# Modulation groups in an attention stage: 64 matmuls moved to GpSimd arithmetic and two partition sums

## The reference

```
def modulation(cond, w_mod, b_mod):            # w_mod: 1024 x 6144
    m = jnp.einsum('bd,df->bf', jax.nn.silu(cond), w_mod) + b_mod
    return jnp.split(m[:, None, :], 6, axis=-1)
```

## Time and profile before

| | |
|---|---|
| median of 3 runs | 2192.92 us (2191.78 to 2200.79) |
| span of the profiled execution | 2192.0 us (the median of the runs is 0.9 us more) |
| TensorE busy | 2040.4 us, 93% |
| VectorE, ScalarE busy | 862.2 us (39%), 470.0 us (21%) |
| GpSimd busy | 154.5 us (7%), 147 instructions |
| mean granted clock of TensorE | 0.963 of full speed |
| the attention | 478 us to 849 us of the span |

### The profile page before, as it was taken

How to read it: one execution, slowest core, us unless ns; L and a number is a source line. 1 busy time by engine, 2 the same in 40 slices (tenths; PEclk the granted TensorE clock), 3 DMA queues, 4 the chain that set the end, 5 groups by cost and what they waited for, 6 DMA issues and landing times. The chain is left out here.

```text
span 2192.0 us, 27484 instructions
## 1 busy us (share of the span) xinstructions
PE 2040.4 (93%) x11455; PEld 1433.7 (65%) x11455; DVE 862.2 (39%) x1806; ACT 470.0 (21%) x927; POOL 154.5 (7%) x147
## 2 busy tenths in 40 slices
PE   5999999979999999999799999995998399999998
PEld 2776777755666665443587878782444387878785
DVE  2245345455666664337222222222546622222222
ACT  1222222126666563113000000001222100000000
POOL 0000000000000000001111111111000101111110
PEclk8999999989999999999899999997899699999999
DMA  9201111048544323753767878766221796878782
GB/s 355 91 25 48 41 44 41 25 108 272 182 178 167 135 97 107 274 170 140 269 235 259 304 259 301 253 214 227 84 82 72 261 343 239 302 260 303 260 287 61
DMA packets 159085, 404.29 MB, mean 184 GB/s; under 512 B 12561, under 2 KB 30664, under 8 KB 152818
## 3 DMA queue, kind: packets, MB, share of 16 engines
q1 hardware_dynamic: 142370, 344.30, 43.6%
q0 software_dynamic: 16592, 58.24, 9.2%
HBM read 339.46 MB, written 63.05 MB: 184 GB/s over the span
## 5 line engine op out<-in xcount | busy, mean ns | idle before, releaser
L1970 PE MATMUL experts_gu<-experts_h_t,shared_w_gate 128*128 128x160 f32 x2048 | 302.7, 301 | 4.1 <-issue 4.1
L1970 PEld LDWEIGHTS experts_gu<-experts_h_t,shared_w_gate 128*128 128x128 f32 x2048 | 288.7, 192 | 19.2 <-issue 19.2
L1970 PE MATMUL experts_gu<-experts_h_t,shared_w_up 128*128 128x160 f32 x2048 | 300.3, 300 | 0.0
L1970 PEld LDWEIGHTS experts_gu<-experts_h_t,shared_w_up 128*128 128x128 f32 x2048 | 286.6, 191 | 0.0
L2046 DVE TENSOR_TENSOR experts_hid<-experts_act,experts_gu 128x160 f32<-128x160 f32 x128 | 41.1, 321 | 479.4 <-ACT experts_act L2035 479.4
L1994 PE MATMUL experts_dn<-shared_w_down,experts_hid 128*128 128x512 f32 x512 | 225.8, 594 | 0.0
L523 PE MATMUL proj_cv<-proj_h_t,proj_w_in 128*128 128x256 f32 x960 | 214.0, 381 | 2.6 <-DVE proj_h_t L720 2.6
L2035 ACT ACTIVATE experts_act<-experts_gu 128x160 f32<-128x160 f32 x128 | 38.8, 303 | 813.4 <-PE experts_gu L1970 813.4
L523 PEld LDWEIGHTS proj_cv<-proj_h_t,proj_w_in 128*128 128x128 f32 x960 | 182.8, 192 | 29.3 <-issue 4.7
L1994 PEld LDWEIGHTS experts_dn<-shared_w_down,experts_hid 128*128 128x128 f32 x512 | 94.7, 190 | 113.8 <-issue 113.8
L1008 PE MATMUL attn_sc<-attn_keys_s,attn_q_s 96*128 96x512 f32 (+1 forms) x384 | 154.6, 539 | 3.8 <-DVE attn_pr_t L1141 2.8
(11 more groups left out here) (407 smaller groups left out, 2122.1 us busy)
## 6 DMA issues: line engine op xcount, KB each, us to landing
shared_w_gate<-w_gate_l SPq DMA_DIRECT2D x32, 2048.0 KB, 9.6
shared_w_up<-w_up_l SPq DMA_DIRECT2D x32, 2048.0 KB, 17.3
shared_w_down<-w_down_l SPq DMA_DIRECT2D x32, 2048.0 KB, 22.7
attn_w_mod<-w_mod_l SPq DMA_DIRECT2D x40, 1024.0 KB, 6.4
proj_w_in<-w_in_l SPq DMA_DIRECT2D x3, 2048.0 KB, 19.7
proj_x<-x POOLq DMA_DIRECT2D x10, 512.0 KB, 3.9
shared_w_down<-x SPq DMA_DIRECT2D x10, 512.0 KB, 4.4
layer_room_a<-w_mod_l SPq DMA_DIRECT2D x4, 1024.0 KB, 10.2
```

What stands on the lines that cost most here:

```text
L1970: last = pe.matmul(gu[j % 2][:, m * SLOTS:(m + 1) * SLOTS], w[u][:, k, j * P:(j + 1) * P], h_t[u][:, k, :], start=(k == 0), stop=(k == KD ...
```

## The change

Groups 3 and 4, (1, 1) and (1, 2), are no longer computed by steps of TensorE. GpSimd loads their blocks from its own DMA queue to two new buffers `w_sum`, multiplies each block by the column of conditioning values (a scalar for each partition) once for each of the two conditioning vectors, and adds the products up over the eight blocks to two sums of 128 x 2048: for a group 16 multiplications and 14 additions. TensorE then only sums the partitions of the two sums: `reduce`, eight matmuls of 512 columns with a stationary tile of 128 x 2 that holds ones in one column and zeros in the other, so that both sums land in the same rows as the steps' results did.

The reductions stand in slots 42 and 66, the turns of these groups in slots 44 and 68. Steps and turns of groups 0 to 2 stay where they were, and slots 39 to 57 lose their steps and turns. The sum of group 4 waits at its first block until the reduction of group 3 has read the sums (`sums_used`). The weights of the steps have two buffers in place of four, and VectorE writes four small columns of the selecting tile at the start.

```
--- before.py
+++ after.py
@@ -166,8 +166,10 @@
 
     WIDE, Q, R = 2048, 4, 32
 
-    def __init__(self, s, t, per, groups, bank, buffers, w=None, rows=2):
+    def __init__(self, s, t, per, groups, bank, buffers, w=None, rows=2, summed=()):
         self.t, self.per, self.groups, self.bank, self.NB = t, per, groups, bank, buffers
+        self.summed = list(summed)
+        self.stepped = [i for i in range(len(groups)) if i not in self.summed]
         self.w = w or [s.sb(f"w_mod{b}", [P, self.WIDE])[:] for b in range(buffers)]
         self.bias = [s.sb(f"mod_bias{u}", [P, BANK]) for u in range(rows)]
         self.rows = [s.sb(f"mod_rows{u}", [P, BANK]) for u in range(rows)]
@@ -175,7 +177,56 @@
         self.w_used, self.rows_ready, self.rows_out = s.sem("w_mod_used"), s.sem("mod_rows_ready"), s.sems("mod_rows_out", 2)
         self.zeroed, self.full = s.sem("mod_zeroed"), s.sem("mod_full")
         self.turned, self.columns = s.sem("mod_turned"), s.sem("mod_columns")
-        self.steps = KD * len(groups)
+        self.steps = KD * len(self.stepped)
+        if self.summed:
+            self.ws = [s.sb(f"w_sum{b}", [P, self.WIDE]) for b in range(2)]
+            self.sums = [s.sb(f"mod_sum{c}", [P, self.WIDE]) for c in range(2)]
+            self.scaled = s.sb("mod_scaled", [P, self.WIDE])
+            self.pick = s.sb("mod_pick", [P, 2, 2])
+            self.ws_in, self.sum_chain, self.sums_used = s.sems("w_sum_in", 2), s.sem("mod_sum_chain"), s.sem("mod_sums_used")
+            self.picked = s.sem("mod_picked")
+
+    def load_sum(self, pool, n):
+
+        if n < KD * len(self.summed):
+            (layer, g), k, b = self.groups[self.summed[n // KD]], n % KD, n % 2
+            pool.dma_start(self.ws[b][:], self.t[f"w_mod_l{layer}"][k * P:(k + 1) * P, g * self.WIDE:(g + 1) * self.WIDE]).then_inc(self.ws_in[b], 16)
+
+    def add_up(self, pool):
+
+        ch = Chain(pool, self.sum_chain)
+        for n in range(2):
+            self.load_sum(pool, n)
+        for n in range(KD * len(self.summed)):
+            j, k, b = n // KD, n % KD, n % 2
+            pool.wait_ge(self.ws_in[b], 16 * (n // 2 + 1))
+            if k == 0:
+                wait(pool, self.sums_used, j)
+            if k == 0:
+                for c in range(2):
+                    ch.add(pool.tensor_scalar(self.sums[c][:], self.ws[b][:], self.per.cond[:, k, c:c + 1], None, ALU.mult))
+                ch.settle()
+            else:
+                for c, scaled in ((0, self.scaled), (1, self.ws[b])):
+                    ch.link(pool.tensor_scalar(scaled[:], self.ws[b][:], self.per.cond[:, k, c:c + 1], None, ALU.mult))
+                    ch.add(pool.tensor_tensor(self.sums[c][:], self.sums[c][:], scaled[:], ALU.add))
+                ch.settle()
+            self.load_sum(pool, n + 2)
+
+    def reduce(self, pe, i):
+
+        j = self.summed.index(i)
+        pe.wait_ge(self.sum_chain, (4 * KD - 2) * (j + 1))
+        if j == 0:
+            pe.wait_ge(self.zeroed, 1 + len(self.bias))
+            pe.wait_ge(self.picked, 2)
+        wait(pe, self.rows_ready, i)
+        wait(pe, self.columns, self.turns_before(i))
+        for c in range(2):
+            for q in range(self.Q):
+                last = pe.matmul(self.bank[self.R * q:self.R * q + 2, :], self.pick[:, c, :], self.sums[c][:, q * BANK:(q + 1) * BANK],
+                                 start=(c == 0), stop=(c == 1), skip_group_check=True)
+        last.then_inc(self.sums_used, 1)
 
     def turns_before(self, i):
         return sum(1 for group in self.groups[:i] if self.wants_columns(group))
@@ -186,7 +237,7 @@
 
     def load(self, sp, n):
         if n < self.steps:
-            (layer, g), k, b = self.groups[n // KD], n % KD, n % self.NB
+            (layer, g), k, b = self.groups[self.stepped[n // KD]], n % KD, n % self.NB
             wait(sp, self.w_used, n - self.NB + 1)
             sp.dma_start(self.w[b], self.t[f"w_mod_l{layer}"][k * P:(k + 1) * P, g * self.WIDE:(g + 1) * self.WIDE]).then_inc(self.w_in[b], 16)
 
@@ -213,9 +264,14 @@
         dve.memset(self.bank, 0.0).then_inc(self.zeroed, 1)
         for u in range(len(self.bias)):
             dve.memset(self.bias[u][:], 0.0).then_inc(self.zeroed, 1)
+        if self.summed:
+            for c in range(2):
+                for m in range(2):
+                    last = dve.memset(self.pick[:, c, m:m + 1], 1.0 if c == m else 0.0)
+                last.then_inc(self.picked, 1)
 
     def step(self, pe, n):
-        i, k, b = n // KD, n % KD, n % self.NB
+        i, k, b = self.stepped[n // KD], n % KD, n % self.NB
         pe.wait_ge(self.w_in[b], 16 * (n // self.NB + 1))
         if k == 0:
             if i == 0:
@@ -235,7 +291,10 @@
             last.then_inc(self.turned, 1)
 
     def add_bias(self, dve, i):
-        dve.wait_ge(self.w_used, KD * (i + 1))
+        if i in self.summed:
+            dve.wait_ge(self.sums_used, self.summed.index(i) + 1)
+        else:
+            dve.wait_ge(self.w_used, KD * (self.stepped.index(i) + 1))
         dve.wait_ge(self.bias_in[i % 2], 16 * self.Q * (i // 2 + 1))
         if i >= 2:
             dve.wait_ge(self.rows_out[i % 2], 16 * self.Q * (i // 2))
@@ -897,7 +956,7 @@
         o_sb = [s.sb(f"o_sb{u}", [P, BANK]) for u in range(2)]
         sc = [s.ps(f"sc{b}", len(SPANS)) for b in range(2)]
         o_ps = s.ps("o")
-        mod = Modulation(s, t, per, [(0, 1), (0, 2), (1, 0), (1, 1), (1, 2)], s.ps("mod")[:], 4)
+        mod = Modulation(s, t, per, [(0, 1), (0, 2), (1, 0), (1, 1), (1, 2)], s.ps("mod")[:], 2, summed=(3, 4))
 
         vp_in, ks_in, vs_in = s.sem("vp_in"), s.sem("ks_in"), s.sem("vs_in")
         qs_in, o_out = s.sems("qs_in", 2), s.sems("o_out", 2)
@@ -921,10 +980,17 @@
         def last_pair(g):
             return 2 * g + 1 if g < 2 else (g - 1) * (HEADS // 2) + HEADS // 2 - 1
 
+        REDUCED_AT = {42: 3, 66: 4}
+
         def mod_tasks(n):
 
-            i, k = divmod((n - HEADS) // 2, KD // 2 + 1)
-            if n < HEADS or n % 2 == 0 or i >= len(mod.groups):
+            k = (n - HEADS) // 2
+            if n in REDUCED_AT:
+                return [("reduce", REDUCED_AT[n])]
+            if n - 2 in REDUCED_AT:
+                return [("turn", REDUCED_AT[n - 2])]
+            i, k = divmod(k, KD // 2 + 1)
+            if n < HEADS or n % 2 == 0 or i >= len(mod.stepped):
                 return []
             return [("step", KD * i + 2 * k), ("step", KD * i + 2 * k + 1)] if k < KD // 2 else [("turn", i)]
 
@@ -969,7 +1035,7 @@
                     for task, m in mod_tasks(n):
                         if task == "step":
                             mod.load(sp, m + mod.NB)
-                        else:
+                        elif task == "turn":
                             mod.store(sp, m)
                             mod.load_bias(sp, m + 2)
                     if n >= 2 and n % 2 == 0 and n // 2 - 1 == last_pair(group(n // 2 - 1)):
@@ -1054,10 +1120,16 @@
                     for task, m in mod_tasks(n):
                         if task == "step":
                             mod.step(pe, m)
+                        elif task == "reduce":
+                            mod.reduce(pe, m)
                         else:
                             mod.turn(pe, m)
                     if n + 2 < SLOTS_N:
                         scores(n + 2)
+
+            @block.gpsimd
+            def _(pool):
+                mod.add_up(pool)
 
             @block.scalar
             def _(act):
@@ -1154,6 +1226,8 @@
                     for task, m in mod_tasks(n):
                         if task == "step" and m % KD == KD - 1:
                             mod.add_bias(dve, m // KD)
+                        elif task == "reduce":
+                            mod.add_bias(dve, m)
                     if n + 2 < SLOTS_N:
                         guard(n + 2)
```

## The result

| | before | changed |
|---|---|---|
| median of 5 runs | 2192.92 us (2188.87 to 2200.79) | 2236.98 us (2233.63 to 2246.74) |
| ratio | | 1.0196, 95% interval 1.0172 to 1.0220 |
| span of the profiled execution | 2192.0 us | 2237.4 us |
| the attention, from its first matmul to the next stage's | 851.81 - 478.46 = 373.35 us | 895.81 - 478.31 = 417.50 us |

The kernel got slower by 44 us, and the attention alone by 44.15 us. The forecast was 2188.3 us with a range from 2185.5 to 2206.

The account below looks back on a forecast made before the run. TensorE, busy 93% of the span, was taken to bound the kernel. Span 2192.0 - 6.1 (TensorE's work) + 1.5 (transfers at the start) = 2187.4, plus 0.9 for the median: 2188.3 us, range 2185.5 to 2206.

Parts of the forecast that it names:

- TensorE's balance: TensorE in the attention: 10.9 us of steps removed, 3.7 us of reductions and 1.1 us of turns added, sum -6.1 us.
- The deadline: GpSimd's sum of group 4 has 116.7 us between the two reductions; anything beyond stops TensorE in slot 66.
- the start: First transfers of the attention: GpSimd's blocks beside the keys and the steps' blocks, taken to cost TensorE 1.5 us.
- The addition: One GpSimd addition of 128x2048 f32, priced at twice VectorE's 2.3 us: 4.6 us, 14 per group.
- The multiplication: One GpSimd multiplication by a column of scalars, 128x2048 f32, priced at VectorE's 2.3 us, 16 per group.
- high end: GpSimd's group with all 30 operations at twice VectorE's price, 4.6 us each, plus 7.5 us: 146 us; value taken 109.
- rival 4: Transfers at the attention's start cost 4 to 7 us in place of 1.5: kernel 2191 to 2194 us; chance 0.09.
- The two buffers: Step weights in two buffers, not four: loads hidden, cover 1.5 us at the worst, a miss costing that much each time.
- Rival 2: GpSimd multiplications cost 4.6 us like additions, group 146 us, TensorE stops 29 us in slot 66: 2218 us; chance 0.11.
- Rival 3: GpSimd and VectorE hinder each other in SBUF: one group up to 272 us, kernel 2405 us; chance 0.03.

## Why the prediction was wrong, point by point

- **TensorE's balance** was right: odd slots without steps take 3.90 us, a reduction 1.83, a turn 0.50 (0.56 forecast); 6.3 us gained where 6.1 were forecast, and 6.4 when measured alone.
- **The deadline** was right: 116.7 us forecast between the reductions, 116.3 measured. So was the place where it would show, slot 66. The 123 us a group at which the gain would be used up left out the 1.5 us of the start; with them it is 121.
- **The addition** was right: 4.6 us forecast, 4.53 measured.
- **The multiplication** is the step that failed. "Value taken: twice for the additions [...] and once for the multiplications, which fetch one": 2.3 us, with 4.6 as the high end. It takes 5.44 us. 16 x (5.44 - 2.3) = 50 us is all of the 48 by which the group's 157 exceed the 109 (additions, issues and handovers came out 2 us below their forecast). The high end of 146 us was itself too low, and the range of the time ended at 2206, that is at 134 us a group, with a chance of 0.14 left above it. My reasoning, that the price goes with the number of tensors fetched, is contradicted by the instruction itself: with one tensor and one operation it is dearer than the addition of two. With the multiplications at 1.98 us and nothing else changed the wait in slot 66 is gone. The rule that I quoted beside it, that one-input operations run roughly at line rate (the Trainium skill, GPSIMD Engine Reference, "Engine selection"), holds here for a copy (1.89 us) and for the instruction with two operations (1.90 to 2.04), near the 1.7 us worked out from it, and fails for the instruction with one (5.44). The 4.5 us that the Trainium skill has for the addition (the same page, "Elementwise — side-by-side cycle accounting") agree with the 4.53 measured.
- **The start** was mis-sized: "I take 1.5 us, nearer to nothing"; 8.1 were lost, more than the 4 to 7 of rival 4. I had priced the delay of transfers and not what the wait does to the clock: 3.46 us are waiting for the keys, and nearly all the rest is score matmuls and transposes at 1.2 GHz behind it (the first twelve score matmuls 2.9 us, the transposes 1.3 us longer than before). The wait came at the keys, which I had with 5 us of room, and not at the steps' blocks. There the two queues share the full DMA engines (share 1.13 from 508 to 512): SyncE's ten issues of keys take 22.1 us in place of 16.0, the last key block is issued at 499.5 and has landed at about 511.5, 12 us later, where in the kernel before it was issued at 493.6 and took 8.8. With GpSimd's loads held back the loss was gone, and arithmetic without loads caused none.
- **The two buffers** of the steps, taken as nothing with "1.5 us at the worst" of cover, cost nothing that shows in the changed kernel, and up to 4.3 us where GpSimd's first loads fell on them.
- **Rival 2** (multiplications as dear as additions, at 2218 us) had the mechanism that came; I gave it 0.11. With 5.44 in place of 4.6 (13 us) and the start (6.6) it is 2238, the result.
- **Rival 3** (GpSimd and VectorE in each other's way) is refuted: in the 40 us in which VectorE stands idle GpSimd's multiplications take 5.43 to 5.45 us as at all other times and its additions 4.49 against 4.53; VectorE is busy for 862.3 us where it was 862.2; and the arithmetic alone changed the kernel's time by a ratio of 1.0010 (0.9991 to 1.0029).

## What to carry to other kernels

When work goes to an engine that has shown none of it in the trace, another engine's rows don't price it: here they were out by a factor of 2.4 (2.3 us against 5.44). Measure the single instruction in the form in which it is used, before the order is built on it, and put the high end of the range beyond the nearest row by more than feels necessary. Work that is off the path needs a deadline for each piece, not one for the sum: here GpSimd had 337 us (487 to 824, when TensorE is ready for the second sum) for 314 us of work, and still stopped TensorE for 41, because the second half could not begin before the first had been read. And a task goes where its engine waits anyway: the same reduction costs 1.37 us in an odd slot and 1.83 in an even one, a turn nothing or 0.50.

## What the runs showed of the hardware that I had not expected

- GpSimd's instruction on a 128x2048 f32 tile and scalars takes 5.36 us (a constant) or 5.44 (a column; multiplied or as a maximum) with one operation. With two operations it takes 1.90 us (two constants), 1.98 (a column and a constant) or 2.04 (two columns).
- The addition of two different tiles of that size takes 4.53 us there, and a product 3.60 if the second operand is a repeated column or the same tile.
- A wait of TensorE of 3.46 us, early in the stage, was followed by about 10 us at half the clock (0.88 from 510 to 514, 0.50 from 514 to 522, 0.84 from 522 to 526); in the 40.8 us of the second wait it fell to 0.50 as well, and the reduction behind it took 3.48 us instead of 1.83.
